# Page rows of a paged attention issued from GpSimd instead of SyncE, with a page-number load of their own

## What is computed

```python
past_c = cache_kv_latent[l, page_table].reshape(DB, past_len, KV_RANK)      # 16 pages of 128 x 256 per sample
past_pe = cache_k_rope[l, page_table].reshape(DB, past_len, QK_ROPE)
s_past = einsum('bqhr,bkr->bhqk', q_abs, past_c) + einsum('bqhd,bkd->bhqk', q_pe, past_pe)
s = concatenate([s_past, s_new], axis=-1) * MLA_SCALE
p = softmax(where(visible, s, -inf), axis=-1)
o = einsum('bhqk,bkr->bqhr', p[..., :P], past_c) + einsum('bhqk,bkr->bqhr', p[..., P:], kv_c)
```

## Time and profile before

| | |
|---|---|
| median of 3 runs | 2500.71 us (2500.01 to 2503.49) |
| the profiled execution | 2504.96 us |
| its span | 2503.2 us |
| busy share of the span: PE, DVE, ACT, POOL | 94%, 57%, 32%, 25% |
| attention loop, first page scores to last output transposes | 466.82 to 648.58 us |
| row issues, column issues | 128 of 128 KB, 128 of 192 KB, all by SP |

### The profile page before, as it was taken

How to read it: one execution, slowest core, us unless ns; L and a number is a source line. 1 busy time by engine, 2 the same in 40 slices (tenths; PEclk the granted TensorE clock), 3 DMA queues, 4 the chain that set the end, 5 groups by cost and what they waited for, 6 DMA issues and landing times.

```text
span 2503.2 us, 47100 instructions
## 1 busy us (share of the span) xinstructions
PE 2342.7 (94%) x18227; PEld 2281.6 (91%) x18227; DVE 1424.5 (57%) x2037; ACT 792.7 (32%) x1155; POOL 628.2 (25%) x260
## 2 busy tenths in 40 slices
PE   7999998676799988999999999999999999999996
PEld 7999997455699987999999999999999999999996
DVE  6332467667533445988888888884333333333366
ACT  5222331122311333544444444443222222222210
POOL 3334353000044331300000000003343343343342
PEclk9999999788899999999999999999999999999998
DMA  5222252477422241333333333336323233233222
GB/s 232 93 85 84 96 170 77 148 232 241 172 94 85 83 177 68 130 125 124 126 123 124 124 123 125 127 110 235 114 97 120 82 129 119 84 128 119 92 84 88
DMA packets 102470, 312.28 MB, mean 125 GB/s; under 512 B 12449, under 2 KB 45250, under 8 KB 99714
## 3 DMA queue, kind: packets, MB, share of 16 engines
q1 hardware_dynamic: 98640, 293.19, 34.8%
q10 hardware_dynamic: 3762, 18.21, 1.9%
HBM read 284.40 MB, written 26.94 MB: 124 GB/s over the span
## 4 chain that ended last, share of the span: by engine, by line
PE 56%; issue 33%; POOL 10%; DVE 1%; POOLq 0%; ACT 0%; DVEq 0%; ACTq 0%
PE psum L2275 31%; PE psum L2225 25%; POOL hl L485 10%; DVE x L1765 0%; PE psum L2245 0%; DVE rstd_x L1033 0%; POOLq L484 0%; POOLq L488 0%; DVE up_units L1588 0%; DVE hidden_out L1575 0%; DVE hl L1604 0%; DVE hl_sums L1604 0%; PE psum L1808 0%; ACT hl_sums L879 0%; DVE hl_blocks L1597 0%
## 5 line engine op out<-in xcount | busy, mean ns | idle before, releaser
L485 POOL TENSOR_TENSOR hl<-raw,hl 128x1024 fp32r<-128x1024 f32 x256 | 628.0, 2454 | 1844.0 <-ACT hl L973 1102.1
L2275 PE MATMUL psum<-hidden_split,hl 128*128 128x272 f32 x6144 | 776.7, 289 | 1.9 <-ACT half_sum L927 1.7
L2275 PEld LDWEIGHTS psum<-hidden_split,hl 128*128 128x128 f32 x6144 | 776.1, 188 | 2.5 <-DVE hidden_split L1649 1.9
L1778 PE MATMUL psum<-xg,hl 128*128 128x272 f32 x4128 | 527.6, 290 | 32.2 <-DVE xg L1028 20.1
L1778 PEld LDWEIGHTS psum<-xg,hl 128*128 128x128 f32 x4128 | 523.7, 191 | 35.4 <-POOL hl L485 21.6
L973 ACT CAST hl<-raw 128x1024 fp32r<-128x1024 f32 x128 | 134.7, 1052 | 590.6 <-PE psum L2275 586.4
L1741 DVE TENSOR_TENSOR x<-x,psum 128x544 f32<-128x544 f32 x112 | 80.8, 722 | 400.4 <-PE psum L2275 398.9
L2225 PE MATMUL psum<-x_terms,hl_blocks 128*128 128x272 f32 x1890 | 266.8, 288 | 0.0
L2225 PEld LDWEIGHTS psum<-x_terms,hl_blocks 128*128 128x128 f32 x1890 | 248.8, 188 | 0.0
L516 ACT CAST hl<-raw 128x1024 fp32r<-128x1024 f32 x100 | 104.5, 1047 | 349.7 <-PE psum L1778 269.9
L2225 PE MATMUL psum<-x_terms,hl 128*128 128x272 f32 x1440 | 190.0, 287 | 0.0
(11 more groups left out here) (299 smaller groups left out, 2391.0 us busy)
## 6 DMA issues: line engine op xcount, KB each, us to landing
raw<-in_w_stream SPq DMA_DIRECT2D x256, 512.0 KB, 3.5
up_units<-in_w_stream SPq DMA_DIRECT2D x120, 512.0 KB, 3.4
page_cols<-in_pool_t SPq DMA_DIRECT2D x128, 192.0 KB, 3.7
h_keep<-hidden_out SPq DMA_DIRECT2D x32, 544.0 KB, 2.9
page_rows<-in_pool_n SPq DMA_DIRECT2D x128, 128.0 KB, 2.4
hidden_in<-h_keep SPq DMA_DIRECT2D x7, 2176.0 KB, 7.7
x<-in_x_t ACTq DMA_DIRECT2D x4, 1088.0 KB, 11.9
out<-x SPq DMA_DIRECT2D x8, 544.0 KB, 2.7
```

The source lines that it names most:

```text
L485: nc.gpsimd.tensor_tensor(HL[s % 2][:, 1, :, :], RAW[:, s, :, :], HL[s % 2][:, 0, :, :].bitcast(F32), ALU.subtract).then_inc(w_lo, 1)
L1778: last = mm(PSUM[:, s + half, 0:HALF], HL[slot][:, wp, blk, :], src[:, xp, k, HALF * half:HALF * (half + 1)], start=start and n == 0, stop ...
L2275: last = mm(PSUM[:, b + half, 0:HALF], HL[t % 2][:, wp, k, :], HT[par][k][:, xp, HALF * half:HALF * half + HALF], start=k == 0 and n3 == 0 ...
```

## The change

The row issues leave SP's program. SP now runs, per batch: wait for `kt_used`, 16 column issues, the next page numbers. POOL's loop over the weight units is cut into three parts: units 0 to 73, then a loop over the 8 batches that loads the batch's page numbers into POOL's registers, waits for `pvs` and issues the 16 rows, then units 74 onwards as before. The waits for the page table and for `w_used` stand ahead of POOL's loop. The order of the work on PE, VectorE and ScalarE stays as it was.

```diff
@@ SP
-                if b == 0:
-                    sp.wait_ge(w_used, U_KV)
-                next_pages = page_numbers(b + 1) if b < NB - 1 else None
-
-                sp.wait_ge(pvs, b + 1)
-                for g in range(PAGES):
-                    sp.dma_start(NAT[:, g, :], pool_n[bass.ds(pages_of[g], 1), :, :]
-                                 .rearrange("a p n -> (a p) n")).then_inc(ld_nat, 16)
-                pages_of = next_pages
+                if b < NB - 1:
+                    pages_of = page_numbers(b + 1)
@@ POOL
-            with pool.Fori(0, U_SEVEN // 4) as i:
+            with pool.Fori(0, U_OUT // 4) as i:
+                for s in range(4):
+                    unit_low(i, s)
+            unit_low(U_OUT // 4, 0)
+            unit_low(U_OUT // 4, 1)
+
+            pool.wait_ge(ld_pg, 16)
+            pool.wait_ge(w_used, U_KV)
+            with pool.Fori(0, NB) as b:
+                _, rows_of = nc.values_load_multi_w_load_instructions(
+                    PTAB[0:1, bass.ds(b * PAGES, PAGES)], engines=[mybir.EngineType.Pool], min_val=0,
+                    max_val=pool_n.shape[0] - 1)
+                pool.wait_ge(pvs, b + 1)
+                for g in range(PAGES):
+                    pool.dma_start(NAT[:, g, :], pool_n[bass.ds(rows_of[g], 1), :, :]
+                                   .rearrange("a p n -> (a p) n")).then_inc(ld_nat, 16)
+
+            unit_low(U_OUT // 4, 2)
+            unit_low(U_OUT // 4, 3)
+            with pool.Fori(U_OUT // 4 + 1, U_SEVEN // 4) as i:
                 for s in range(4):
                     unit_low(i, s)
```

## The result

The changed kernel takes **2509.9 us** (median of 7 runs, 2504.59 to 2511.61); the kernel before, on the same chip and between those runs, 2503.3 us (median of 7, 2500.01 to 2504.32). The ratio is 1.0021, with a 95% interval of 1.0012 to 1.0031 (the two medians alone would give 1.0026): some 3 to 8 us slower, just beyond the 0.2% bound in the middle of the interval and not at its lower end. The forecast was 2510 us.

A forecast was written before the change was run, and what follows sets the result against it. Bound: a chain passing from engine to engine, no engine full, transfers not setting turn length. Waits of 6.45 us (last turn) and 2.7 us, plus up to 3 for number loads, taken as 9.5, on 2500.71 gave 2510 us; range 2499 to 2532.

The forecast's parts named there:

- The price c: POOL's cost per row issue: 1.10 us, between 0.503 and 2.39, plus 0.06 for VectorE's interference, giving 1.16 us.
- rival A: POOL issues nearly as cheaply as SP, c below 1.07 us: not slower, 2500.7 to 2505.5 us; chance 0.30.
- once over 5 us: Sign of being right: PE's value matmuls wait for row transfers once over 5 us, in the last turn.
- under 2 us elsewhere: Sign of being right: PE's waits for row transfers outside the last turn stay under 2 us.
- the 2.7 us for batches 1 to 6: PE's summed waits for late rows before the value matmuls of batches 1 to 6: 2.7 us together.
- the pitch under 0.75 us: Sign of wrong size: POOL's row issues under 0.75 us apart, with no new PE wait for rows.
- The landing: After an issue on POOL ends, a row takes 2.07 us to land (2.4 less 0.333), left as on SP.
- Columns sooner, worth 0: SP issues page columns some 8 us sooner each turn; they were never late, so worth 0.
- batch 0, covered: Batch 0's rows: POOL is free at 459.00 and 31 us remain to 490.74, so they arrive in time.
- The number load: POOL's load of page numbers, up to 5.26 us; if not overlapped, 0.4 us a turn, 3 us at most.
- Rival B: VectorE holds POOL's issues off in full: c 1.34 us, 28.6 us lost, 2529 us; with dearer issues, chance 0.20.
- Rival C: Faster by clock: six attention turns all as short as the shortest gain 4.3 us, under 0.2%; chance 0.05.

The follow-up runs named there:

- half the room: Changed kernel with half the SBUF memory for GpSimd's transfer lists (8 KiB a partition instead of 16); 2503.07 us, one run.
- rows after columns: Changed kernel, but POOL begins its row loop only when batch 0's columns have landed; 2507.57 us, ratio 1.0017.
- the changed one with the earlier splits: Changed kernel, with ScalarE making upper halves of weight units 72 and 73 ahead of its wait for the absorbed queries; 2499.98 us, ratio 0.9984.
- twice the issues: Changed kernel, but each page row comes in two transfers of half its width, 256 issues on POOL; 2533.89 us, ratio 1.012.
- the first experiment: Changed kernel, but SP issues the last batch's rows and POOL only batches 0 to 6, 112 issues; 2505.81 us, ratio 1.0008.
- the last two: Changed kernel with ScalarE's early halves of units 72 and 73: 2499.98 us; that plus last batch on SP and batch 0's rows held back: 2495.54 us.
- the second and the fourth experiment: Changed kernel with batch 0's rows held until its columns landed, 2507.57 us; changed kernel with SP issuing 2 of each batch's 16 rows, 2506.64 us.

## Why the prediction was right, and where it was not

The time, its direction and the place of the loss came out as forecast: slower, with one wait for rows, in the last turn, and none for columns within the turns. The loss is smaller than forecast, some 6 us where the sum had 9.5, and the kernel before measured 2503.3 here where the sum started from 2500.7; the two make up for each other in the 2510. **And the step that gave the size was wrong, and something else filled its place: that the number holds is luck.**

*The price c.* It was taken as 1.16 us, and it is 0.585: the term was mis-sized by a factor of two. It lies next to the lower bound, SP's 0.503 us (0.514 by the same working as POOL's, 8.05 less 0.333 by 15), far from the 2.39 us of a split; the middle in ratio between the two ends had no ground but their being far apart, and the remark that the instruction is the same as SP's was the better guide. With 0.585 us the prediction's own sum gives 16 times 0.585 plus 2.07, 11.4 us, against 14.18 us at hand in the last turn. Nothing would have been late anywhere, and the answer would have been 2500.7, that is, rival A. The "once over 5 us" in the last turn was 3.3, and the "under 2 us elsewhere" were none at all: the 2.7 us for batches 1 to 6 did not come as waits for rows. Of the prediction's own signs of being wrong in size, the pitch under 0.75 us is there; the entry in PE's waits is there all the same, but not from the price.

From the first-byte times of the Trainium skill, "DMA: Bandwidth & Descriptors", section "Latency and other measured facts", the prediction had an estimate of 0.84 us for an issue. Their order, GpSimd's path dearer than SP's, agrees with 0.585 against 0.514; the ratio of the two first-byte times does not carry over to the pitch.

*The landing.* It was left at SP's 2.4 us after the issue. The median of POOL's rows was 4.5 us, as they now travel beside SP's columns, and those went from 3.7 us at the median to 6.6 between 476 and 625 us. In the last pass, where no columns are under way, the last 15 rows took 2.3 to 2.7, so in the one turn that counted the term was right.

*What made the rows late instead.* The pause of 3.4 us ahead of the 114th issue. No row of the kernel before hints at it, since POOL issues nothing there. Three runs show it as a matter of count and room: 112 issues have none, half the room moves it to the 57th, and 256 issues meet it at the 114th and the 227th. That it hits the second issue of the last pass, in the one turn with the least time over, is chance: in a middle turn it would have been hidden, as it was with half the room.

*The clock behind the wait.* The prediction counted a wait at its length. PE got 1.2 us back, because its last head values happened to run in 2.49 us; but the value matmuls behind the wait took 2.84 us, at a mean grant of 0.65 where before they took 1.93 at 1.00. In the three kernels with one transfer per row where PE stood idle for 2.4 us or more ahead of them (the changed one, rows after columns, and the changed one with the earlier splits) they were slow (2.84, 2.49 and 3.38 us for idle times of 3.26, 2.92 and 2.40); with no wait for rows, or one of 1.17 us (half the room), they took 1.93 us. The length of the wait alone does not decide it: with twice the issues they took 1.93 us behind waits of 1.99 to 2.55 us, and 3.64 and 3.43 us behind those of 7.77 and 11.70.

*Columns sooner, worth 0.* Right within the turns: SP stands idle for them, and no wait of PE was there to be shortened. But the step looked at PE's waits from 490 us on, and the first columns' wait lies at 466. There the change has a cost that the prediction did not have: "batch 0, covered" counted only whether its rows are in time, not that they now run beside the columns of batch 0 that PE is waiting for. Holding them back returned that wait from 9.4 to 8.2 us.

*The number load.* POOL's first issue starts 2.24 us after its split ends, and that contains the load; later passes load the numbers while POOL waits for PE. The 3 us allowed for it were not needed. SP's weight unit and the splits behind the loop cost next to nothing, as said (first split at 675.58, 28.33 us after the last issue, released by ScalarE; PE's wait for the splits went from 2.79 to 2.95 us).

*Rival B, VectorE holding POOL off.* It falls. The median issue took 538 ns and the longest 741, and that is close to the 0.69 us of the first issue of the program; 16 issues took 9.48 to 9.69 us in every pass without a pause, though VectorE was at work for about 16 us of each turn. The Trainium skill, "SBUF — State Buffer", section "Who interferes with whom", has VectorE in a two-port mode shutting GpSimd out, so that GpSimd cannot write its descriptors. Whether VectorE was in that mode here no run shows; the mean issue took 554 ns where the shortest took 538, which is 0.26 us over 16 issues, and more than that it did not cost in a pass.

*Rival C, the clock.* The length of the six turns went from 137.1 to 141.4 us over kernels with no wait for a transfer in them, and it goes with the number of turns at the higher clock: 137.1 and 137.2 with four, 138.1 to 139.1 with three, 139.5 and 139.7 with two, 141.4 with one. What decides which turns these are, no experiment here asked. In the changed kernel this was worth 2.35 us of the 6.25, on the losing side. So the measured slowdown is the pause (some 3 us by the first experiment's ratio, some 4.5 by the last two), the rows of batch 0, and where the turns fall on the clock. How the last two share the rest is open: the second and the fourth experiment removed a cause each, and got back about 1 and 2 us, with intervals as wide as that.

A forecast of 2510 that holds, with a price that is off by two, is a warning: the price made the sum too high, the losses left out made it too low, and the two happened to come out near each other.

## What to carry to other kernels

Count the issues that move to GpSimd as well as their price: here one costs 0.585 us whatever its bytes, hardly more than on SP, but after 113 of them the engine stopped once for 3.5 us, and it matters in which pass that falls. Moving an issue is worth something only where its queue was what somebody waited for; ask first which transfer PE really waits for, over the whole stretch and not from the first steady turn on. Here that was one wait of 8 us ahead of the loop, and a change of three lines on another engine took it away and gained 8 us, 0.34%.

## What the runs showed of the hardware

GpSimd issues a transfer of 128 row pieces every 0.585 us (0.54 us busy), for pieces of 256 and of 128 numbers alike; SP's pitch for the same rows was 0.514 us. The first issue of the program took 0.69 us, and the second came 0.98 us after it.

The engine pauses when the room reserved for its transfers has been filled: ahead of the 114th issue with the usual room, of the 57th with half of it, and of the 114th and 227th where there are 256. Its idle time there was 3.2 to 6.6 us, and the profile gives no reason for it but "issue". A larger room was not tried.

The landings show what goes with the length. The row issued last before the pause, in the changed kernel (the 113th) and with half the room (the 56th), each with the time from its issue to its landing:

```profile
L495 POOL DMA_DIRECT2D page_rows<-in_pool_n x1: 538/538/538, 634.5 to 634.5; - x1
...
DMA to landing us min/median/max: 2.4/2.4/2.4
...
L495 POOL DMA_DIRECT2D page_rows<-in_pool_n x1: 678/678/678, 545.2 to 545.2; - x1
...
DMA to landing us min/median/max: 5.5/5.5/5.5
```

The 113th landed at 636.9 (634.48 plus 2.4), and the 114th was issued at 638.51, 1.6 us later. The same 1.6 us stand between that landing and the next issue in the other four pauses with the usual room: the rows after the columns, the earlier splits, and both with twice the issues, where the idle times were 6.58 and 3.15 us. With half the room it is about 1 us (550.7 to 551.64). So POOL went on a fixed time after the landing of the last row issued, and the pause is as long as that landing makes it. This fits the short second pause with half the room: the last row issued before it had landed at 627.0 (620.63 plus 6.3), some 7 us before POOL comes to the next row in a usual pass, 3 us after the value matmuls (630.92). It is read from these pauses; no experiment changed the landing alone.

The Trainium skill has figures that meet here. "DMA: Bandwidth & Descriptors" gives a descriptor as a struct of 16 bytes (section "Terms") and 9 of them per DMA engine for a transfer of 1 MiB to 128 partitions (section "The descriptor swizzle"), and "SBUF — State Buffer" gives 16 KiB a partition for GpSimd's descriptors (section "SBUF size: 192, 224, or 256?"). As an estimate from these, 16384 bytes by 144 is 113.8, so 113 transfers fit and the 114th does not; 8192 by 144 is 56.9. The runs agree with both.
